# A hybrid decoder layer on one core: the first transfers of three stages reordered and split, and a reciprocal root taken as an exponential of a logarithm

## Chip, core and metric

One core of a Trainium2 chip. The metric is the device time of the whole program in microseconds (us), median of three runs. Engines: TensorE (PE, with its weight loads PEld), VectorE (DVE), ScalarE (ACT), GpSimd (POOL), and SyncE (SP), which issues all the DMAs that are spoken of here.

## What is computed

One layer on x of 2048 tokens by 1024 channels, and a final norm:

```python
h = rms_norm(x, norm_mix); proj = h @ w_in
o_a = gated linear attention; o_b = RG-LRU branch; o_c = dilated attention, then rms_norm
x = x + concatenate([o_a, o_b, o_c]) @ w_out
h = rms_norm(x, norm_ffn)
up = causal_dwconv(h @ ffn_w_up, ffn_conv_w, ffn_conv_b)
u_val, u_gate = split(up)
x = x + (u_val * gelu(u_gate)) @ ffn_w_down
return rms_norm(x, norm_final)       # x * rsqrt(mean(x*x) + EPS) * g
```

## The kernel before

Four stages follow each other: `mixer_front` (input projection, groups A and B), `dilated_attention` (group C), `output_projection` and `conv_ffn`. Each ends with a barrier of all engines, at which every DMA of the stage has landed; then the next stage's queues start. Within a stage every engine runs a list written out by hand, in order, and waits on semaphores. Data are held transposed, channels on the 128 partitions, and tokens come in four blocks of 512 (`NB`). All large products have float32 accuracy through splits: ACT copies an operand to `_hi`, DVE subtracts to get `_lo`, and PE makes three passes (L66 to L68; in the FFN L2035 to L2037) per 128 by 128 piece of weights and 512 tokens. The names begin with the stage: ip_, at_, op_, ff_.

**`dilated_attention`.** SP loads q, k and v of a block (`load_qkv`, L1292, 768 KB each), two identities (`idb`, `idf`), the masks, and then the other blocks. PE waits at its start for both identities and the masks, and at the first scores for q, k and v of block 0. `idf` and v are first used in `turn_values` (L1609), after the three score groups of the first tile.

**`output_projection`.** The weights come in four slabs of 256 columns (1 MB each, `w_raw`, two buffers), the mixed input in tiles of 128 by 512 (256 KB) through a ring of four (`mix_in`, `load_mix`, L1828). ACT makes `w_hi` of slab 0 (L1874), then `mix_hi` of the eight tiles of block 0 (L1882); DVE follows with `w_lo` (L1934) and `mix_lo` (L1939), which also frees a ring slot for SP. The first product (m = 0) waits for one `mix_lo` after the other. DVE adds each product to x (L1992), with four PSUM banks, so product n waits for addition n - 4; in each block DVE makes the next block's `mix_lo` of the same index first. ACT squares the sum, POOL adds the squares, PE sums over partitions, ACT takes the square root (`root`, L1894), and DVE the reciprocal (`invert`, L1944) into `rstd`, for blocks 0 to 2 in the middle of the next block, for block 3 at the stage's end. DVE then norms blocks 0 and 1 and forms differences of them (`norm`, `combine`) for the FFN, and stores go out to `h_t`.

**`conv_ffn`.** The up-projection uses a Strassen scheme of seven products for each of 22 slabs; the tokens are done in two halves of 1024. `ORDER` names products: A00, S1, S2, A01, S3, A00 of the next slab, A11, A01 of the next, S4, and so on. At the start SP loads seven inputs `b_raw` (1 MB each) from `h_t` and slab 0 (1 MB) after the first of them; ACT makes `b_hi` of one input and then one weight piece (`high_b`, `high_w`), seven times, and only after these the copies of product results (`keep`, L2448) that S2 waits for. Product A00 waits for all four pieces of its input. Between the halves, and at the end, comes the final norm of a half: squares, totals, `root(half, b)` for its two blocks (ACT square root, L2490), `invert(half)` on DVE (reciprocal L2645, then four multiplications L2649 per block), and stores. Between the halves PE goes on with products of half 1; its S4 waits for two moves on DVE (`move`, L2597, L2599), which wait for the four stores of half 0 (`late_stored`); A11 waits for ACT's copy of S3. At the end POOL multiplies the other half of the channels (L2408) beside DVE.

## Time and profile before

| | us |
|---|---|
| median of 3 runs (lowest, highest) | 2625.37 (2622.48, 2629.85) |
| profiled execution, own time | 2634.46 |
| span of the profiled execution | 2632.7 |
| PE busy | 2482.2 (94%) |
| DVE / ACT / POOL busy | 1582.7 / 1074.8 / 735.1 |

The profiled execution's time is 1.8 us more than its span. A row of the timeline gives the start from the span's beginning, the duration, and in brackets how long the engine sat idle before it and what released it. Matmuls are pipelined, so one of 0.39 us starts 0.23 us after the one before at full clock, and one of 0.63 us 0.43 us after it at half clock.

### The profile page before, as it was taken

The numbers are of one execution on the slowest core, as the hardware profiler recorded it, in microseconds if no ns is written. First come the engines' busy times: TensorE is split into PE (matmuls) and PEld (weight loads), VectorE is DVE, ScalarE is ACT, GpSimd is POOL, SyncE is SP. The second block draws the span as 40 slices with busy tenths as digits, with TensorE's granted clock in tenths as the row PEclk, the third lists the DMA queues.
The fourth block names the chain that finished last, engine by engine and source line by source line (L and its number), as shares of the span: only waits on it lengthen the run. The fifth ranks groups of instructions, "written<-read, shape, count | busy, mean of one in ns | idle before, by whom it ended". The sixth has DMA issues, their size and how long they took to land.

```text
span 2632.7 us, 32946 instructions
## 1 busy us (share of the span) xinstructions
PE 2482.2 (94%) x12224; PEld 2003.0 (76%) x12224; DVE 1582.7 (60%) x2166; ACT 1074.8 (41%) x1847; POOL 735.1 (28%) x648
## 2 busy tenths in 40 slices
PE   7999999999799996995999999899989999989995
PEld 5777777777578775874888888788868888878884
DVE  7554447774355674455777777445577877763435
ACT  6434353332146553213444444225444444432422
POOL 4111103331003770323333333012044534310103
PEclk9999989999899998997999999999999999999997
DMA  4232224442513325364212122365413222225472
GB/s 160 97 111 93 94 87 156 143 148 72 191 59 127 103 71 212 108 228 180 88 72 93 76 88 85 140 211 201 163 73 131 102 88 81 86 83 175 146 242 109
DMA packets 147199, 327.27 MB, mean 124 GB/s; under 512 B 12624, under 2 KB 54624, under 8 KB 139104
## 3 DMA queue, kind: packets, MB, share of 16 engines
q1 hardware_dynamic: 147040, 325.17, 35.4%
q8 instruction: 98, 1.61, 0.3%
q14 instruction: 61, 0.50, 0.1%
HBM read 231.55 MB, written 93.57 MB: 123 GB/s over the span
## 4 chain that ended last, share of the span: by engine, by line
PE 46%; DVE 3%; ACT 1%; DMA 1%; issue 1%; POOL 1%; SPq 0%; DVEq 0%; ACTq 0%; POOLq 0%
PE ff_bank L2035 16%; PE ff_bank L2037 15%; PE ff_bank L2036 15%; DVE ff_y L2618 1%; POOL ffn_rstd L2362 1%; DMA ff_b_raw<-h_t 1%; DVE ff_x2d L2649 1%; DVE ffn_rstd L2645 1%; DMA ff_a_raw<-a_t 0%; ACT ff_y L2457 0%; ACT ff_b_hi L2420 0%; DVE ff_x2d L2640 0%; DVE ff_a_lo L2632 0%; ACT ff_e L2448 0%; ACT ff_ring L2438 0%
## 5 line engine op out<-in xcount | busy, mean ns | idle before, releaser
L2035 PE MATMUL ff_bank<-ff_b_hi,ff_ring 128*128 128x512 f32 x1232 | 483.5, 392 | 37.3 <-DVE ff_ring L2580 15.8
L2036 PE MATMUL ff_bank<-ff_b_lo,ff_ring 128*128 128x512 f32 x1232 | 482.0, 391 | 0.0
L2037 PE MATMUL ff_bank<-ff_b_hi,ff_ring 128*128 128x512 f32 x1232 | 482.0, 391 | 0.0
L66 PE MATMUL ip_bank<-ip_x_hi,ip_w_hi 128*128 128x512 f32 x736 | 309.1, 420 | 19.4 <-DVE ip_x_lo L701 16.2
L2035 PEld LDWEIGHTS ff_bank<-ff_b_hi,ff_ring 128*128 128x128 f32 x1232 | 233.1, 189 | 90.4 <-issue 31.7
L67 PE MATMUL ip_bank<-ip_x_lo,ip_w_hi 128*128 128x512 f32 x736 | 298.8, 406 | 0.0
L68 PE MATMUL ip_bank<-ip_x_hi,ip_w_lo 128*128 128x512 f32 x736 | 297.4, 404 | 0.0
L2035 PE MATMUL ff_bank<-ff_a_hi,ff_w_hi 128*128 128x512 f32 x704 | 276.6, 393 | 15.5 <-DVE ff_a_lo L2632 15.4
L2618 DVE SCALAR_TENSOR_TENSOR ff_y<-ff_u,ff_conv_all,ff_y 128x1024 f32<-128x1024 f32 x176 | 240.2, 1365 | 62.8 <-ACT ff_y L2457 59.3
L2036 PE MATMUL ff_bank<-ff_a_lo,ff_w_hi 128*128 128x512 f32 x704 | 275.7, 392 | 0.0
L2037 PE MATMUL ff_bank<-ff_a_hi,ff_w_lo 128*128 128x512 f32 x704 | 275.4, 391 | 0.0
L2037 PEld LDWEIGHTS ff_bank<-ff_b_hi,ff_ring 128*128 128x128 f32 x1232 | 232.9, 189 | 48.7
L2036 PEld LDWEIGHTS ff_bank<-ff_b_lo,ff_ring 128*128 128x128 f32 x1232 | 233.0, 189 | 48.3 <-issue 0.2
L2580 DVE TENSOR_TENSOR ff_ring<-ff_raw,ff_ring 128x512 fp32r<-128x512 f32 x220 | 178.3, 812 | 56.5 <-ACT ff_ring L2438 56.5
L2630 DVE TENSOR_TENSOR ff_w_lo<-ff_w_raw,ff_w_hi 128x512 fp32r<-128x512 f32 x88 | 62.6, 712 | 243.6 <-ACT ff_w_hi L2471 243.6
L66 PEld LDWEIGHTS ip_bank<-ip_x_hi,ip_w_hi 128*128 128x128 f32 x736 | 145.4, 198 | 57.9 <-issue 14.8
L2471 ACT ACTIVATE ff_w_hi<-ff_w_raw 128x512 fp32r<-128x512 f32 x88 | 55.6, 631 | 302.9 <-PE ff_bank L2037 269.9
L67 PEld LDWEIGHTS ip_bank<-ip_x_lo,ip_w_hi 128*128 128x128 f32 x736 | 145.9, 198 | 32.0 <-issue 2.6
L68 PEld LDWEIGHTS ip_bank<-ip_x_hi,ip_w_lo 128*128 128x128 f32 x736 | 145.3, 197 | 32.1
L2035 PEld LDWEIGHTS ff_bank<-ff_a_hi,ff_w_hi 128*128 128x128 f32 x704 | 133.2, 189 | 45.7 <-DVE ff_a_lo L2632 17.5
L2457 ACT ACTIVATE ff_y<-ff_u,ff_conv_all 128x1024 f32<-128x1024 f32 x88 | 109.6, 1245 | 135.6 <-DVE ff_u L2601 101.1
L1440 ACT ACTIVATE at_probs<-at_s,at_neg 128x256 f32<-128x256 f32 (+1 forms) x288 | 107.8, 436 | 137.3 <-DVE at_neg L1521 123.5
(244 smaller groups left out, 4402.2 us busy)
## 6 DMA issues: line engine op xcount, KB each, us to landing
ff_raw<-in_slabs SPq DMA_DIRECT2D x44, 1024.0 KB, 4.8
ff_a_raw<-a_t SPq DMA_DIRECT2D x88, 512.0 KB, 4.1
proj_t<-ip_staged SPq DMA_DIRECT2D x92, 256.0 KB, 2.7
a_t<-ff_y SPq DMA_DIRECT2D x44, 512.0 KB, 2.7
ff_w_raw<-in_w_down SPq DMA_DIRECT2D x88, 256.0 KB, 2.7
rp_tables<-in_rope SPq DMA_DIRECT2D x24, 512.0 KB, 4.5
ip_w_raw<-in_w_in SPq DMA_DIRECT2D x23, 512.0 KB, 4.1
at_qkv<-proj_t SPq DMA_DIRECT2D x12, 768.0 KB, 12.1
```

The source lines that it names most:

```text
L66: pe.matmul(out, w_hi[k], x_hi[k], start=(k == 0), stop=False)
L67: pe.matmul(out, w_hi[k], x_lo[k], start=False, stop=False)
L68: last = pe.matmul(out, w_lo[k], x_hi[k], start=False, stop=(k == n - 1))
L1440: ins = act.activation(probs[:, g, at], scores_at(j, g)[:, hh, n * c:n * (c + 1)], ACT.Exp, bias=neg[:, j % 2, c, 2 * g + hh:2 * g + hh + 1])
L2035: pe.matmul(out, w_hi, x_hi, start=first, stop=False, skip_group_check=resumed)
L2036: pe.matmul(out, w_hi, x_lo, start=False, stop=False, skip_group_check=resumed)
L2037: return pe.matmul(out, w_lo, x_hi, start=False, stop=last, skip_group_check=resumed)
L2457: act.activation(y[:, a, :], u[:, a, TAPS - 1:], ACT.Identity, bias=conv_all[:, g, a, TAPS:TAPS + 1], scale=conv_all[:, g, a, TAPS - 1:TAP ...
L2471: act.activation(w_hi[n % 2][:, :], w_raw[n % 2][:, :], ACT.Copy).then_inc(d_hi_ready, 1)
L2580: dve.tensor_tensor(ring[:, M % RING, 1, :], source(half, m), ring[:, M % RING, 0, :].bitcast(F32), ALU.subtract).then_inc(w_lo_ready, 1)
L2618: dve.scalar_tensor_tensor(out=y[:, a, :], in0=u[:, a, t:t + HALF], scalar=conv_all[:, g, a, t:t + 1], in1=y[:, a, :], op0=ALU.mult, op1=A ...
L2630: dve.tensor_tensor(w_lo[n % 2][:, :], w_raw[n % 2][:, :], w_hi[n % 2][:, :].bitcast(F32), ALU.subtract).then_inc(d_lo_ready, 1)
```

## The change

Attention: the small identity and the masks are loaded first, then q, k, `idf`, v of block 0; PE's start waits for identity and masks, scores for q and k alone, `turn_values` for v and `idf`. Output projection: slab 0 comes in two halves of 128 columns (rows of 512 bytes), each split on its own; ACT and DVE do the first half, two tiles, the second half, then six tiles; product 0 waits for the first half. FFN: weight piece A00 of slab 0 is loaded and split ahead of everything, and products on slab 0 wait for one piece of input after the other. Both norms: ACT takes Ln and then Exp with scale -0.5, which gives the reciprocal root, and DVE's reciprocal is gone. A table set that holds both functions is loaded at the start of the output projection and ahead of the last eight squares.

```diff
@@ -1176,7 +1176,9 @@
         gain_in = sem("gain_in")
-        qkv_in = [sem(f"qkv_in{b}") for b in range(BLOCKS)]
+        mask_in = sem("mask_in")
+        qk_in = [sem(f"qk_in{b}") for b in range(BLOCKS)]
+        values_in = [sem(f"values_in{b}") for b in range(BLOCKS)]
...
 
         @block.sync
         def _(sp):
+            def load_one(b, a, t, landed):
+                sp.dma_start(qkv[:, a, :, blk(b)], proj_t[t:t + GROUPS, :, blk(b)].rearrange("g p s -> p g s")).then_inc(landed[b], 16)
+
             def load_qkv(b):
-                for a, t in enumerate((T_CQ, T_CK, T_CV)):
-                    sp.dma_start(qkv[:, a, :, blk(b)], proj_t[t:t + GROUPS, :, blk(b)].rearrange("g p s -> p g s")).then_inc(qkv_in[b], 16)
+                load_one(b, 0, T_CQ, qk_in)
+                load_one(b, 1, T_CK, qk_in)
+                load_one(b, 2, T_CV, values_in)
...
@@ -1332,10 +1338,12 @@
                 sp.wait_ge(out_ready, 4 * (b + 1))
                 sp.dma_start(mix_t[5:8, :, blk(b)].rearrange("g p s -> p g s"), out[:, b % 2, :, :]).then_inc(out_stored[b % 2], 16)
 
-            load_qkv(0)
-            sp.dma_start(idb[:, :], ident_bf).then_inc(consts_in, 16)
-            sp.dma_start(mask[:, :, :], masks).then_inc(consts_in, 16)
+            sp.dma_start(idb[:, :], ident_bf).then_inc(mask_in, 16)
+            sp.dma_start(mask[:, :, :], masks).then_inc(mask_in, 16)
+            load_one(0, 0, T_CQ, qk_in)
+            load_one(0, 1, T_CK, qk_in)
             sp.dma_start(idf[:, :], ident).then_inc(consts_in, 16)
+            load_one(0, 2, T_CV, values_in)
             sp.dma_start(gain[:, :], swa_gain).then_inc(gain_in, 16)
             for b in range(1, BLOCKS):
                 load_qkv(b)
...
@@ -1373,7 +1381,7 @@
                     pool.wait_ge(scores_ready, GROUPS * (j - 1))
                 elif j == TILES_0:
                     for b in range(BLOCKS):
-                        pool.wait_ge(qkv_in[b], 48)
+                        pool.wait_ge(qk_in[b], 32)
...
 
             def make_diagonal(i):
                 f = i - FIRST_1
+                if f == 0:
+                    pool.wait_ge(consts_in, 16)
                 pool.wait_ge(rstd_ready, f + 1)
...
@@ -1599,10 +1609,14 @@
 
         @block.tensor
         def _(pe):
-            pe.wait_ge(consts_in, 16 * 3)
+            pe.wait_ge(mask_in, 32)
             pe.wait_ge(cleared, 2)
 
             def turn_values(b):
+                if b % 4 == 0:
+                    pe.wait_ge(values_in[b // 4], 16)
+                if b == 0:
+                    pe.wait_ge(consts_in, 16)
                 if b:
                     pe.wait_ge(v_ready, b)
...
@@ -1816,7 +1833,11 @@
             def load_weights(n):
                 if n >= 2:
                     sp.wait_ge(w_ready, n - 1)
-                sp.dma_start(w_raw[:, n % 2, :, :], w_slabs[n]).then_inc(w_loaded[n % 2], 16)
+                if n == 0:
+                    sp.dma_start(w_raw[:, 0, :, 0:P], w_slabs[0, :, :, 0:P]).then_inc(first_loaded, 16)
+                    sp.dma_start(w_raw[:, 0, :, P:2 * P], w_slabs[0, :, :, P:2 * P]).then_inc(w_loaded[0], 16)
+                else:
+                    sp.dma_start(w_raw[:, n % 2, :, :], w_slabs[n]).then_inc(w_loaded[n % 2], 16)
...
@@ -1869,9 +1890,14 @@
 
         @block.scalar
         def _(act):
+            def first_high():
+                act.wait_ge(first_loaded, 16)
+                act.activation(w_hi[:, :, 0:P], w_raw[:, 0, :, 0:P], ACT.Copy).then_inc(first_hi_ready, 1)
+
             def weights_high(n):
                 act.wait_ge(w_loaded[n % 2], 16 * (n // 2 + 1))
-                act.activation(w_hi[:, :, n * 2 * P:(n + 1) * 2 * P], w_raw[:, n % 2, :, :], ACT.Copy).then_inc(w_hi_ready, 1)
+                skip = 0 if n else P
+                act.activation(w_hi[:, :, n * 2 * P + skip:(n + 1) * 2 * P], w_raw[:, n % 2, :, skip:], ACT.Copy).then_inc(w_hi_ready, 1)
...
@@ -1891,10 +1917,15 @@
 
             def root(b):
                 act.wait_ge(sum_done, b + 1)
-                act.activation(rstd[:, blk(b)], sum_bank[:, :], ACT.Sqrt, bias=eps[:, :], scale=1.0 / D).then_inc(std_ready, 1)
-
+                act.activation(rstd[:, blk(b)], sum_bank[:, :], ACT.Ln, bias=eps[:, :], scale=1.0 / D).then_inc(std_ready, 1)
+                act.wait_ge(std_ready, b + 1)
+                act.activation(rstd[:, blk(b)], rstd[:, blk(b)], ACT.Exp, scale=-0.5).then_inc(rstd_ready, 1)
+
+            act.preload_act_table_set("natural_log_exp_and_others")
+            first_high()
+            high(0, range(2))
             weights_high(0)
-            high(0, range(KT))
+            high(0, range(2, KT))
             for n in range(1, OUT_SLABS):
                 weights_high(n)
...
@@ -1928,10 +1959,15 @@
             dve.memset(ones[:, :], 1.0).then_inc(consts_ready, 1)
             dve.memset(eps[:, :], EPS).then_inc(consts_ready, 1)
 
+            def first_low():
+                dve.wait_ge(first_hi_ready, 1)
+                dve.tensor_tensor(w_lo[:, :, 0:P], w_raw[:, 0, :, 0:P], w_hi[:, :, 0:P].bitcast(F32), ALU.subtract).then_inc(first_ready, 1)
+
             def weights_low(n):
                 dve.wait_ge(w_hi_ready, n + 1)
-                at = slice(n * 2 * P, (n + 1) * 2 * P)
-                dve.tensor_tensor(w_lo[:, :, at], w_raw[:, n % 2, :, :], w_hi[:, :, at].bitcast(F32), ALU.subtract).then_inc(w_ready, 1)
+                skip = 0 if n else P
+                at = slice(n * 2 * P + skip, (n + 1) * 2 * P)
+                dve.tensor_tensor(w_lo[:, :, at], w_raw[:, n % 2, :, skip:], w_hi[:, :, at].bitcast(F32), ALU.subtract).then_inc(w_ready, 1)
...
-            def invert(b):
-                dve.wait_ge(std_ready, b + 1)
-                dve.reciprocal(rstd[:, blk(b)], rstd[:, blk(b)]).then_inc(rstd_ready, 1)
-
+            first_low()
+            low(0, 0)
+            low(0, 1)
             weights_low(0)
-            for k in range(KT):
+            for k in range(2, KT):
                 low(0, k)
             for n in range(1, OUT_SLABS):
                 weights_low(n)
...
                     dve.tensor_tensor(at, banks[n % 4][:, :], at, ALU.add).then_inc(added, 1)
-                    if b and m == 2:
-                        invert(b - 1)
                     if b in (1, 2) and m in (3, 4):
                         for k in range(KH * (m - 3), KH * (m - 2)):
                             norm(b - 1, k)
                     if b == 2 and m in (4, 5, 6, 7):
                         for k in range(KH):
                             combine((T1, T3, T2, T4)[m - 4], k)
-            invert(BLOCKS - 1)
             dve.wait_ge(rstd_ready, BLOCKS)
...
@@ -2016,7 +2048,9 @@
                     pe.wait_ge(mix_ready, KT * (b + 1))
                 for m in range(KT):
                     n = KT * b + m
-                    if b == 0 and m % 2 == 0:
+                    if n == 0:
+                        pe.wait_ge(first_ready, 1)
+                    elif b == 0 and (m == 1 or m % 2 == 0):
                         pe.wait_ge(w_ready, m // 2 + 1)
...
@@ -2202,7 +2237,10 @@
                 if G >= 2:
                     before, h = (g - 2, half) if g >= 2 else (g - 2 + PAIRS, half - 1)
                     sp.wait_ge(w_lo_ready, use_at(h, "S4", before) + 1)
-                sp.dma_start(raw[:, g % 2, :, :], slabs[g]).then_inc(slab_in[g % 2], 16)
+                if G == 0:
+                    sp.dma_start(raw[:, 0, 1:4, :], slabs[0, :, 1:4, :]).then_inc(slab_in[0], 16)
+                else:
+                    sp.dma_start(raw[:, g % 2, :, :], slabs[g]).then_inc(slab_in[g % 2], 16)
...
 
+            sp.dma_start(raw[:, 0, 0, :], slabs[0, :, 0, :]).then_inc(first_in, 16)
             load_h(B00)
             load_slab(0, 0)
...
@@ -2424,6 +2465,8 @@
                 G = PAIRS * half + g
                 if name[0] == "S":
                     act.wait_ge(s_ready, 4 * G + int(name[1]))
+                elif G == 0 and name == "A00":
+                    act.wait_ge(first_in, 16)
                 else:
                     act.wait_ge(slab_in[g % 2], 16 * (PAIRS // 2 * half + g // 2 + 1))
...
@@ -2487,14 +2530,19 @@
                 act.wait_ge(sum_done, 2 * half + b + 1)
                 if half and b == 0:
                     act.wait_ge(early_ready, 2 * OC)
-                act.activation(out_rstd[:, blk(b)], banks[SUM[b]][:, :], ACT.Sqrt, bias=eps[:, :], scale=1.0 / D).then_inc(std_ready, 1)
+                act.activation(out_rstd[:, blk(b)], banks[SUM[b]][:, :], ACT.Ln, bias=eps[:, :], scale=1.0 / D).then_inc(std_ready, 1)
+                act.wait_ge(std_ready, 2 * half + b + 1)
+                act.activation(out_rstd[:, blk(b)], out_rstd[:, blk(b)], ACT.Exp, scale=-0.5).then_inc(rstd_ready, 1)
 
             for half in range(HALVES):
                 if half == 0:
                     for i in range(7):
+                        if i == 0:
+                            high_w(0, 0)
                         for k in range(KH):
                             high_b(0, KH * i + k)
-                        high_w(0, i)
+                        if i:
+                            high_w(0, i)
                     act.wait_ge(consts_ready, 2)
...
@@ -2543,6 +2591,7 @@
                     square(0, 1, range(6, 8))
                     high_w(1, 8)
                 else:
+                    act.preload_act_table_set("natural_log_exp_and_others")
                     square(1, 1, range(8))
...
@@ -2641,8 +2690,6 @@
 
             def invert(half):
                 for b in range(HB):
-                    dve.wait_ge(std_ready, 2 * half + b + 1)
-                    dve.reciprocal(out_rstd[:, blk(b)], out_rstd[:, blk(b)]).then_inc(rstd_ready, 1)
                     dve.wait_ge(rstd_ready, 2 * half + b + 1)
                     for o in range(OC):
...
@@ -2652,9 +2699,12 @@
             for half in range(HALVES):
                 if half == 0:
                     for o in range(7):
+                        if o == 0:
+                            low_w(0, 0)
                         for i in range(4 * o, 4 * o + 4):
                             low_b(0, i)
-                        low_w(0, o)
+                        if o:
+                            low_w(0, o)
...
@@ -2713,8 +2763,6 @@
                 G = PAIRS * half + g
                 o, bank, first = {"A00": (B00, X, True), "S1": (T1, Y, True), "S2": (T2, X, False), "A01": (B10, Z, True),
                                   "S3": (T3, X, False), "A11": (T4, X, False), "S4": (B11, Y, False)}[name]
-                if g == 0:
-                    pe.wait_ge(b_lo_ready, 28 * half + 4 * (HI_AT[o] + 1))
                 pe.wait_ge(w_lo_ready, M + 1)
...
                 out = banks[bank[g % 2]][:, :]
                 for k in range(KH):
+                    if g == 0:
+                        pe.wait_ge(b_lo_ready, 28 * half + 4 * HI_AT[o] + k + 1)
                     cols = slice(k * P, (k + 1) * P)
```

SP's queue at the start of the attention; `at_qkv` is the tile of q, k and v. Before:

```order
L1292 DMA at_qkv<-proj_t 128x3x512 x3
L1336 DMA at_idb<-in_ident_bf 128x128
L1337 DMA at_mask<-in_masks 128x768
L1338 DMA at_idf<-in_ident 128x128
L1339 DMA at_gain<-in_swa_norm 128x3
L1292 DMA at_qkv<-proj_t 128x3x512 x9
```

and now:

```order
L1341 DMA at_idb<-in_ident_bf 128x128
L1342 DMA at_mask<-in_masks 128x768
L1293 DMA at_qkv<-proj_t 128x3x512 x2
L1345 DMA at_idf<-in_ident 128x128
L1293 DMA at_qkv<-proj_t 128x3x512
L1347 DMA at_gain<-in_swa_norm 128x3
L1293 DMA at_qkv<-proj_t 128x3x512 x9
```

v of block 0 and `idf` stand behind what PE's first scores need.

ACT between the two halves of the FFN; `ff_e` is a copy of a product, `ff_ring` holds split weights, `ffn_rstd` the reciprocal root. Before:

```order
L2448 ACTIVATE ff_e<-ff_bank 128x512
L2490 ACT_TABLE_LOAD
L2490 ACTIVATE ffn_rstd<-ff_bank,ff_eps 128x512 x2
L2438 ACTIVATE ff_ring<-ff_s_12793 128x512 x2
L2438 ACTIVATE ff_ring<-ff_raw 128x512
L2448 ACTIVATE ff_e<-ff_bank 128x512
```

and now:

```order
L2491 ACTIVATE ff_e<-ff_bank 128x512
L2533 ACT_TABLE_LOAD
L2533 ACTIVATE ffn_rstd<-ff_bank,ff_eps 128x512
L2535 ACT_TABLE_LOAD
L2535 ACTIVATE ffn_rstd<-ffn_rstd 128x512
L2533 ACT_TABLE_LOAD
L2533 ACTIVATE ffn_rstd<-ff_bank,ff_eps 128x512
L2535 ACT_TABLE_LOAD
L2535 ACTIVATE ffn_rstd<-ffn_rstd 128x512
L2481 ACTIVATE ff_ring<-ff_s_12806 128x512 x2
L2481 ACTIVATE ff_ring<-ff_raw 128x512
L2491 ACTIVATE ff_e<-ff_bank 128x512
```

One table load has become four here, since no set is loaded by hand in half 0.

SP's queue at the start of the output projection. Before:

```order
L1819 DMA op_w_raw<-in_w_out 128x2048
L1828 DMA op_mix_in<-mix_t 128x512 x4
L1819 DMA op_w_raw<-in_w_out 128x2048
L1828 DMA op_mix_in<-mix_t 128x512 x4
L1819 DMA op_w_raw<-in_w_out 128x2048
L1836 DMA op_x<-in_x_t 128x8x512
```

and now:

```order
L1837 DMA op_w_raw<-in_w_out 128x8x128
L1838 DMA op_w_raw<-in_w_out 128x8x128
L1849 DMA op_mix_in<-mix_t 128x512 x4
L1840 DMA op_w_raw<-in_w_out 128x2048
L1849 DMA op_mix_in<-mix_t 128x512 x4
L1840 DMA op_w_raw<-in_w_out 128x2048
L1857 DMA op_x<-in_x_t 128x8x512
```

Both halves of slab 0 still stand ahead of the input tiles; nothing behind them has moved.

## Rows read from the trace of the kernel before

**Rows 1.** The page: PE's granted clock in 40 slices of the span, tenths.
```profile
PEclk9999989999899998997999999999999999999997
```

**Rows 2.** Timeline, PE: start, busy us, engine, line, operation; idle before and its releaser.
```profile
701.36 0.61 PE L1627 MATMUL at_s<-at_mask,at_idb 128*128 128x256 bf16 x2 [14.68 <-DMA at_idf<-in_ident]
1022.01 0.77 PE L66 MATMUL op_bank<-op_mix_hi,op_w_hi 128*128 128x512 f32 x1 [15.64 <-DVE op_mix_lo L1939]
1049.09 0.47 PE L66 MATMUL op_bank<-op_mix_hi,op_w_hi 128*128 128x512 f32 x1 [1.73 <-DVE op_x L1992]
1163.34 0.50 PE L66 MATMUL op_bank<-op_mix_hi,op_w_hi 128*128 128x512 f32 x1 [3.38 <-DVE op_mix_lo L1939]
1227.75 0.77 PE L2035 MATMUL ff_bank<-ff_b_hi,ff_ring 128*128 128x512 f32 x1 [15.76 <-DVE ff_ring L2580]
1246.19 0.76 PE L2035 MATMUL ff_bank<-ff_b_hi,ff_ring 128*128 128x512 f32 x1 [10.16 <-ACT ff_e L2448]
1948.24 0.76 PE L2035 MATMUL ff_bank<-ff_b_hi,ff_ring 128*128 128x512 f32 x1 [8.60 <-DVE ff_u L2599]
```

**Rows 3.** Table of windows: span, PE, PEld, DVE, ACT, POOL busy, clock, DMA, GB/s.
```profile
696.00:701.00 5.00, 0.00 (x0) 0.00 (x0) 0.00 (x0) 0.00 (x0) 0.00 (x0) 0.50 1.03 356
```

**Rows 4.** Timeline at the projection's start: ACT, then SP.
```profile
1028.64 0.63 ACT L1882 ACTIVATE op_mix_hi<-op_mix_in 128x512 fp32r<-128x512 f32 x1 [1.33 <-DMA op_mix_in<-mix_t]
1046.91 2.46 ACT L1882 ACTIVATE op_mix_hi<-op_mix_in 128x512 fp32r<-128x512 f32 x4 [4.47 <-DMA op_mix_in<-mix_t]
1021.89 2.12 SPq L1828 DMA_DIRECT2D op_mix_in<-mix_t  x4
```

**Rows 5.** Timeline, DVE in block 2 of the projection.
```profile
1136.13 3.34 DVE L1944 RECIPROCAL ffn_rstd<-ffn_rstd 128x512 f32<-128x512 f32 x1
1143.78 0.68 DVE L1992 TENSOR_TENSOR op_x_third<-op_bank,op_x_third 128x512 f32<-128x512 f32 x1
1144.38 6.03 DVE L1958 SCALAR_TENSOR_TENSOR op_x<-op_x,op_gain,ffn_rstd 128x512 f32<-128x512 f32 x4
1162.61 0.68 DVE L1939 TENSOR_TENSOR op_mix_lo<-op_mix_in,op_mix_hi 128x512 fp32r<-128x512 f32 x1
```

**Rows 6.** Waits of the DMA queue, then DVE's timeline, at the projection's end.
```profile
SPq L1759 <- DMA x_t<-op_x: 6.3, 1, 6.3
1212.75 3.35 DVE L1944 RECIPROCAL ffn_rstd<-ffn_rstd 128x512 f32<-128x512 f32 x1 [3.94 <-ACT ffn_rstd L1894]
```

**Rows 7.** Timeline, ACT at the FFN's start.
```profile
1237.66 2.19 ACT L2420 ACTIVATE ff_b_hi<-ff_b_raw 128x512 fp32r<-128x512 f32 x4 [2.03 <-DMA ff_b_raw<-h_t]
```

**Rows 8.** Timeline, ACT in the mixer: a logarithm, a table load.
```profile
333.53 0.30 ACT L634 ACTIVATE gl_rstd<-gl_ss,ip_eps 128x4 f32<-128x4 f32 x1
333.84 1.28 ACT L636 ACT_TABLE_LOAD   x1
```

**Rows 9.** Timeline between the FFN's halves: ACT, then DVE.
```profile
1927.15 1.28 ACT L2490 ACT_TABLE_LOAD   x1
1931.52 0.60 ACT L2448 ACTIVATE ff_e<-ff_bank 128x512 f32<-128x512 f32 x1 [0.24 <-PE ff_bank L2037]
1938.60 2.74 DVE L2649 SCALAR_TENSOR_TENSOR ff_x2d<-ff_x2d,ff_gain,ffn_rstd 128x512 f32<-128x512 f32 x4
1944.95 0.69 DVE L2597 TENSOR_TENSOR ff_u<-ff_bank,ff_e 128x512 f32<-128x512 f32 x1 [3.01 <-DMA out_t<-ff_x2d]
```

**Rows 10.** Timeline at the end: ACT, DVE, POOL, SP.
```profile
2605.95 1.28 ACT L2490 ACT_TABLE_LOAD   x1
2611.36 5.75 DVE L2649 SCALAR_TENSOR_TENSOR ff_x2d<-ff_x2d,ff_gain,ffn_rstd 128x512 f32<-128x512 f32 x4
2596.83 11.19 POOL L2362 TENSOR_TENSOR ffn_rstd<-ffn_rstd,ff_squares 128x512 f32<-128x512 f32 x8 [94.62 <-ACT ff_squares L2481]
2611.46 6.76 POOL L2408 TENSOR_TENSOR ff_x_last<-ff_x_last,ffn_rstd 128x512 f32<-128x512 f32 x4 [3.44 <-DVE ffn_rstd L2645]
2627.70 0.47 SPq L2297 DMA_DIRECT2D out_t<-ff_x_last  x1
```

More of the change, by code:

```diff
@@ L1462, in stage_queries @@
                     for b in range(BLOCKS):
-                        act.wait_ge(qkv_in[b], 48)
+                        act.wait_ge(qk_in[b], 32)
                 if j >= TILES_0 + 2:
@@ L1616, in scores @@
                         if b % 4 == 0:
-                            pe.wait_ge(qkv_in[b // 4], 48)
+                            pe.wait_ge(qk_in[b // 4], 32)
                     else:
@@ L1788, in output_projection @@
         w_loaded = [sem(f"w_loaded{i}") for i in range(2)]
+        first_loaded = sem("first_loaded")
+        first_hi_ready = sem("first_hi_ready")
+        first_ready = sem("first_ready")
         w_hi_ready = sem("w_hi_ready")
@@ L2114, in conv_ffn @@
         b_lo_ready = sem("b_lo_ready")
+        first_in = sem("first_in")
         slab_in = [sem(f"slab_in{i}") for i in range(2)]
@@ L2323, in sums_of_slab @@
                 pool.wait_ge(slab_in[g % 2], 16 * (PAIRS // 2 * half + g // 2 + 1))
+                if G == 0:
+                    pool.wait_ge(first_in, 16)
                 if G:
```

## Prediction

> **What bounds the kernel now.** I read PE's timeline first, for PE is busy nearly everywhere; what a border costs is an idle stretch ahead of one matmul, and such a stretch names its releaser [rows 2]. Seven of them matter: 14.68 us at the attention's start, 15.64 and then 1.73 in the output projection's first block, 3.38 ahead of its last block, 15.76 and 10.16 at the FFN's start, 8.60 between the halves. After the last matmul comes a tail of DVE, POOL and stores [rows 10]. A first transfer made smaller helps only if nothing behind it is pinned by something else; so for each stretch I ask which arrival ends the next one. The parts below count time saved against the profiled execution, 2634.46 us (its span of 2632.7 and 1.8 around it). It lies 9.1 above the median of 2625.37; the savings are put on both alike.
>
> **Attention's start: 1.9.** PE waits for the last of 2304 KB of q, k, v and 288 KB of identities and masks [rows 2]. Now it waits for 1536 and 224 KB: 832 KB or 0.85 MB less, which at 356 GB/s [rows 3] is 2.4 us. The large transfers stand behind two small ones now; SP needs half a microsecond per issue (four in 2.12) [rows 4], up to 1.0 later in all, partly filled by the small ones. So 1.4 to 2.4, taken 1.9. v and `idf`, landed by about 701.4 as before, are wanted 5 us after the first scores, so at 704: no wait. The stage has no further idle stretch of PE in rows 2, so this passes through.
>
> **Projection's start: -0.6.** Before, PE's first product starts at 1022.01. Half a slab split on its own saves about half of ACT's and DVE's work there, some 2 us, and the product can start near 1020. But its eighth step needs the last input tile, whose load SP issues once DVE has freed a slot with the fourth `mix_lo`; SP's four loads end at 1024.0 and ACT gets that tile at 1028.64 [rows 4]. In the new order the second half of the slab (about 1.0 on ACT and 1.2 on DVE, half of what the whole took) stands ahead of the third and fourth tile, so that load goes out about 1 us later, not earlier. Behind it, product 4 is pinned: it starts at 1049.09 after 1.73 of waiting for an addition [rows 2], which on DVE stands behind a `mix_lo` of block 1, whose tile ACT waited for until 1046.91 [rows 4]. That tile comes after 10 MB of other loads, which the earlier start of PE doesn't hasten, and the loads behind the last tile start later too. Ends: 0.5 saved (the transfers ahead move up a little) to 1.3 lost (the whole delay reaches the pinned tile). Taken: 0.6 lost. The table load at the stage's start stands in ACT's wait for the slab and costs nothing; with PE's start at stake it would cost 1.28.
>
> **Ahead of the last block: 1.8.** PE waits 3.38 for the last `mix_lo` of block 3, at 1162.61 on DVE [rows 2, 5], and DVE works almost without a pause from the reciprocal up to it. The reciprocal of 3.34 at 1136.13 leaves that chain. What is late next: the addition of product 4, at 1143.78. Products end 5.44 apart (24 matmuls, 0.227 each), the last of the block at 1163.34 - 3.38 = 1159.96, so product 4 at 1143.64, and the addition can't move up by more than 0.1. What is left is indirect: the last tile's load also waited for DVE, so ACT's squares and POOL's additions begin some 3 us earlier and run less beside the four multiplications at 1144.38, which took 6.03 there and 2.74 where POOL is quiet [rows 5, 9]. Less than the 3.29 of that excess goes. Bounds 0.1 and 3.3, taken 1.8, the middle. The reciprocals of the other blocks lie in DVE time that PE doesn't wait for in rows 2.
>
> **Projection's end: 0.4.** The reciprocal [rows 6] runs from 1212.75 to 1216.10; an Exp on ACT of about 0.6 (an ACT pass over 512 columns takes 0.60 [rows 9]) takes its place, 2.7 less. But SP waits 6.3 for the last store of x2, issued until 1209.4, so until 1215.7 [rows 6]: what is late next. Bounds 0.3 to 0.4.
>
> **FFN's start: 0.** Product A00 gets its weights and first input piece earlier, by some 3 us. S2 doesn't: it waits for ACT's copy, which stands behind all seven inputs, and ACT waited 2.03 for the sixth until 1237.66 [rows 7], the seventh megabyte in the queue. The same bytes stand ahead of it after the change. PE's gap of 10.16 grows by what the gap of 15.76 loses. Cost up to 0.4, for one more DMA issue.
>
> **Between the halves: 3.5.** Before: two roots, then DVE's reciprocal and multiplications twice, ending at 1941.34; the store lands and the first move starts at 1944.95 [rows 9]; S4 runs at 1948.24. Now four table loads. One load before a logarithm runs 1.28 from 1927.15, and in the mixer a load begins 0.01 after the logarithm of 0.30 before it has ended [rows 8, 9]. So Ln 1928.45 to 1929.14, load, Exp to 1931.1, load, Ln, load, Exp to 1935.0 (0.69, 1.30, 0.62 and so on). DVE's second group of 2.74 ends at 1937.8, that is 3.5 earlier, and store, moves and S4 follow. What is late next: ACT's copy of S3 slips from 1931.52 to 1936.7, ready at 1937.3. A11 would have started at about 1934.1, waits 3.2, and the two products behind it end at 42.9, still before S4's new start of 1944.7. If the clock falls to 1.2 GHz in that wait, as it was after the stretches of 8.60 and more (first matmul 0.76, and 0.50 after 3.38 [rows 2]), they end near 1946.3 and 1.6 is lost. Bounds 1.9 to 3.9.
>
> The Trainium skill, page ScalarE: Activation LUTs, section What ACT_TABLE_LOAD costs, says that every switch costs a drain of about 1.38 us beside the 1.283. Rows 8 show no such gap; by the page the three added switches would take some 4.1 us more (an estimate), and this term would be near -0.6.
>
> **The tail: 6.1.** The table load behind the squares [rows 10] moves ahead of them into idle time, and Exp follows Ln: Ln 2605.95 to 2606.64, Exp to 2607.3; DVE's multiplications begin at 2607.35, not 2611.36 (4.0). Then no reciprocal stands between DVE's groups. POOL becomes the bound: its totals end at 2608.02 [rows 10], then eight multiplications at the 1.65 of its first four (6.76 together) [rows 10], until 2621.3. The last store goes out at 2621.4 instead of 2627.70: 6.3, less 0.2 because eight stores of 512 KB now fall closer. Bounds 4.0 (only the earlier start counts) and 6.5.
>
> **Sum.** 1.9 - 0.6 + 1.8 + 0.4 + 0 + 3.5 + 6.1 = 13.1 us. Profiled 2634.46 - 13.1 = 2621.4; median 2625.37 - 13.1 = **2612.3 us**. About 0.3%, or 7.9 us, is what a measurement of this kernel can tell from no change, so 2617.5 is the border.
>
> **Rivals.**
> - *The first starts pass through.* Projection +2.5, last block 3.3, FFN's start 2.9, the other terms at their better ends (2.4, 0.4, 3.9, 6.5): 21.9, time 2603.5. For it: PE does start earlier at all three. Against: the pinned arrivals of rows 4 and 7. 12%.
> - *The gains are small.* All terms at their worse ends: 1.4 - 1.3 + 0.1 + 0.3 - 0.4 + 1.9 + 4.0 = 6.0, time 2619.4. For it: DVE and POOL slow each other at the tail. 19%.
> - *A switch of tables costs twice its row* where activations depend on each other: three loads more at 1.3 each. DVE ends at 1941.7, the half border gives -0.4, sum 9.2, time 2616.2. Rows 8 speak against it. The page named above would have it so. 6%.
> - *Slower: the clock.* In a slice of the mixer the granted clock lies between 0.8 and 0.9 (the sixth digit, 329 to 395 us), in the attention's middle, 750 to 980, at 0.9 or more [rows 1]. If the shifted start gave the attention's 280 us a clock of 0.85, PE would need 49 us more, net 36 slower, 2648. It decides for slower beyond 0.3% below about 0.93 (280 us x 0.075 = 21). Nothing in the steady part is changed, so 3%.
>
> **Chances.** The forecast has 60%, its own range 2608 to 2617. Faster than 2617.5: the forecast, the first rival, two thirds of the third, and some of the second: 0.82. Within 0.3%: 0.15. Slower: 0.03. The range for 8 in 10 goes from 2606.0, leaving out most of the first rival, to 2619.5, which takes in the second.
>
> **What would show it.** PE's first scores 12 to 13 us after the mixer's last matmul; the projection's first product 2 us earlier but product 4 where it was relative to the stage's start; the stretch of 3.38 down to 1 to 2; S2 of slab 0 still 29 us after SP's first FFN load, with an idle stretch near 13 ahead of it; four loads of 1.28 between the halves, A11 waiting about 3, S4 3.5 earlier; DVE and POOL working side by side from 2608 to the end. I am wrong if product 4 or S2 move up with their starts, if the last block's stretch is gone or untouched, or if the table loads show gaps around them.

## The result, and the profile after

| | us |
|---|---|
| changed kernel, median of 22 runs | 2619.55 (2608.52 to 2629.14) |
| kernel before, the same comparison, 22 runs | 2633.83 (2622.48 to 2640.6) |
| ratio, 95% interval | 0.9946 (0.9934 to 0.9958) |
| profiled execution after: time, span, granted clock | 2608.52, 2606.7, 0.971 |
| profiled execution before: time, span, granted clock | 2634.46, 2632.7, 0.963 |

By the ratio the change saves 0.54% or 14.2 us (11.1 to 17.4); the forecast of the saving was 13.1. The forecast of the time was 2612.3 with a range to 2619.5, and the median is 2619.55. So the saving was met and the time was not, by 0.05 us beyond the range and 7.3 above the forecast: the kernel before reads 2633.83 in this comparison, 8.5 us above the 2625.37 on which the forecast stood. One later execution, of the kernel `combined` below, had a granted clock of 0.741 from end to end and took 3133 us; it is left out of every number here.

The two profiled executions differ by 26.0 us, far more than the ratio. The largest part of that is no work of the change. The table of windows (start and end, span, PE's busy time and instructions, clock, DMA share, GB/s) shows the mixer from 100 us to its last matmul, before and then after, and its code is the same in both:

```profile
100.00:686.68 586.68, 585.67 (x2928) 0.95 0.33 108
```
```profile
100.00:670.36 570.36, 567.86 (x2924) 0.98 0.35 111
```

16.3 us at a clock of 0.95 against 0.98, with PE busy nearly throughout. Whoever compares stages has to count from a mark inside each stage. PE's timeline of the changed kernel, with the rows that answer to [rows 2]:

```profile
683.40 0.58 PE L1641 MATMUL at_s<-at_mask,at_idb 128*128 128x256 bf16 x2 [13.04 <-DMA at_qkv<-proj_t]
1002.83 0.76 PE L66 MATMUL op_bank<-op_mix_hi,op_w_hi 128*128 128x512 f32 x1 [14.36 <-DVE op_mix_lo L1975]
1030.31 0.47 PE L66 MATMUL op_bank<-op_mix_hi,op_w_hi 128*128 128x512 f32 x1 [1.07 <-DVE op_x L2027]
1143.36 0.50 PE L66 MATMUL op_bank<-op_mix_hi,op_w_hi 128*128 128x512 f32 x1 [2.19 <-DVE op_mix_lo L1975]
1207.15 0.77 PE L2069 MATMUL ff_bank<-ff_b_hi,ff_ring 128*128 128x512 f32 x1 [13.54 <-DVE ff_b_lo L2624]
1228.44 0.76 PE L2069 MATMUL ff_bank<-ff_b_hi,ff_ring 128*128 128x512 f32 x1 [8.69 <-issue]
1919.94 0.47 PE L2069 MATMUL ff_bank<-ff_b_hi,ff_ring 128*128 128x512 f32 x1 [3.00 <-issue]
1927.62 0.47 PE L2069 MATMUL ff_bank<-ff_b_hi,ff_ring 128*128 128x512 f32 x1 [1.98 <-DVE ff_ring L2629]
```

The wait of 3.00 ahead of A11 (1919.94) is new, and S4 (1927.62) waits 1.98 instead of 8.60. Between the halves ACT, then DVE:

```profile
1909.92 1.28 ACT L2533 ACT_TABLE_LOAD   x1
1911.22 0.69 ACT L2533 ACTIVATE ffn_rstd<-ff_bank,ff_eps 128x512 f32<-128x512 f32 x1
1911.92 1.28 ACT L2535 ACT_TABLE_LOAD   x1
1913.22 0.64 ACT L2535 ACTIVATE ffn_rstd<-ffn_rstd 128x512 f32<-128x512 f32 x1
1913.87 1.28 ACT L2533 ACT_TABLE_LOAD   x1
...
1915.88 1.28 ACT L2535 ACT_TABLE_LOAD   x1
```
```profile
1917.84 2.74 DVE L2696 SCALAR_TENSOR_TENSOR ff_x2d<-ff_x2d,ff_gain,ffn_rstd 128x512 f32<-128x512 f32 x4 [1.21 <-ACT ffn_rstd L2535]
1924.36 0.69 DVE L2646 TENSOR_TENSOR ff_u<-ff_bank,ff_e 128x512 f32<-128x512 f32 x1 [3.19 <-DMA out_t<-ff_x2d]
```

They answer to [rows 9]. Each load begins within 0.02 us of the end of what stands before it, and the next function begins 0.02 after the load's 1.28. The drain of 1.38 us per switch that the Trainium skill states (page ScalarE: Activation LUTs, section What ACT_TABLE_LOAD costs) isn't on this chain, with each function depending on the one before: the trace disagrees. The tail, DVE, POOL and SP, answering to [rows 10]:

```profile
2588.25 13.05 DVE L2696 SCALAR_TENSOR_TENSOR ff_x2d<-ff_x2d,ff_gain,ffn_rstd 128x512 f32<-128x512 f32 x8 [6.43 <-ACT ffn_rstd L2535]
2589.03 13.39 POOL L2449 TENSOR_TENSOR ff_x_last<-ff_x_last,ffn_rstd 128x512 f32<-128x512 f32 x8
2602.45 0.37 SPq L2336 DMA_DIRECT2D out_t<-ff_x_last  x1
```

DVE and POOL work side by side to the end, at 1.63 and 1.67 us per tile, and the last store is issued as POOL ends.

### The profile page after: what moved, and what is told of

It reads as the page before. It is cut to its first block, busy times and chain, and to the rows that moved or that the text cites. A ratio compares the mean times of both kernels' runs of the same rounds, so it can differ in the third digit from the quotient of the medians.

```text
span 2606.7 us, 32959 instructions
## 1 busy us (share of the span) xinstructions
PE 2468.8 (95%) x12224; PEld 1991.9 (76%) x12224; DVE 1557.8 (60%) x2159; ACT 1083.9 (42%) x1859; POOL 736.3 (28%) x648
## 4 chain that ended last, share of the span: by engine, by line
PE 47%; DVE 3%; POOL 1%; ACT 1%; DMA 1%; issue 1%; SPq 0%; POOLq 0%; ACTq 0%; DVEq 0%
PE ff_bank L2069 16%; PE ff_bank L2071 16%; PE ff_bank L2070 16%; DVE ff_y L2667 1%; POOL ffn_rstd L2403 1%; DVE ff_b_lo L2624 1%; POOL ff_x_last L2449 0%; DMA ff_a_raw<-a_t 0%; DMA ff_b_raw<-h_t 0%; ACT ff_y L2500 0%; DVE ff_ring L2629 0%; DVE ff_x2d L2689 0%; DVE ff_a_lo L2681 0%; ACT ff_a_hi L2515 0%; DMA out_t<-ff_x2d 0%
## 5 line engine op out<-in xcount | busy, mean ns | idle before, releaser
L66 PE MATMUL ip_bank<-ip_x_hi,ip_w_hi 128*128 128x512 f32 x736 | 302.2, 411 | 19.5 <-DVE ip_x_lo L701 16.1
L67 PE MATMUL ip_bank<-ip_x_lo,ip_w_hi 128*128 128x512 f32 x736 | 292.5, 397 | 0.0
L68 PE MATMUL ip_bank<-ip_x_hi,ip_w_lo 128*128 128x512 f32 x736 | 291.4, 396 | 0.0
```

The lines of the kernel that those rows point to most:

```text
L66: pe.matmul(out, w_hi[k], x_hi[k], start=(k == 0), stop=False)
L67: pe.matmul(out, w_hi[k], x_lo[k], start=False, stop=False)
L68: last = pe.matmul(out, w_lo[k], x_hi[k], start=False, stop=(k == n - 1))
```

## The experiments

Each run left a profile, and every kernel has one form or the other of each border, so the borders can be read in many executions. All stretches below are counted from a mark in the same profile. T1 is the matmul between the halves that waits for POOL's total (1924.90 before, 1907.68 after), T2 the first such one at the end (2602.54 and 2583.58). In brackets stand the number of profiles and the range.

| us | as before | as changed |
|---|---|---|
| attention's first scores, behind the mixer's last matmul | 14.61 (4 profiles, 14.48 to 14.68) | 13.07 (9, 12.65 to 13.82) |
| projection: product 0, behind SP's first issue | 10.07 (5, 9.90 to 10.24) | 8.89 (8, 8.45 to 9.33) |
| projection: product 4, behind the same | 37.49 (5, 37.10 to 37.97) | 37.12 (8, 36.08 to 38.05) |
| idle ahead of the last block | 3.33 (3, 3.23 to 3.38) | 2.18 (9, 2.18 to 2.19) |
| FFN: S2, behind SP's first issue | 28.99 (5, 28.95 to 29.05) | 29.99 (7, 29.67 to 30.66) |
| FFN: in the first down stage, the matmul behind PE's wait of some 7 us, to the same one of half 1 ("down stage" below) | 688.5 (3, 688.1 to 688.9) | 685.9 (9, 684.7 to 687.1) |
| end of the span, behind T2 | 30.12 (3, 30.10 to 30.16) | 23.12 (9, 23.06 to 23.15) |

**1. The kernel before, again** (no edit).

> The kernel before, once more. Theory A (the level of a time is set by the clock that an execution happens to get, and the three times shown before the prediction were low ones): ratio 1.000 within 0.001, median between 2628 and 2638 and not 2625; in its profile the mixer, whose code no kernel changes, ends anywhere between 670 and 687 us (670.4 after the change, 686.7 before it), its granted clock going the other way. Theory B (the changed kernel also speeds up the mixer): the mixer ends at 686 to 687 again, and the median is near 2625 plus nothing.

Ratio 1.0001 (0.999 to 1.0013), median 2635.05 of 12 runs. Its mixer ended at 683.1. In all profiles of the study, the mixer, unchanged in every kernel, ended between 670.4 and 686.7. Over the 73 executions of the kernel before that came after the three shown, the median is 2633.3, and only 14 are as low as the highest of those three (2629.85). Theory A stands against Theory B. That all three were low by chance alone would happen about once in 140 times (14/73 three times over, an estimate), so why they were low isn't shown.

**2. The changed kernel, again** (no edit).

> The changed kernel, once more. Theory A: ratio 0.9946 within 0.001; the mixer ends anywhere between 670 and 687 us. From stage to stage, as in its first profile: first scores 13.0 us after the mixer's last matmul, product 4 of the projection 46.1 us after attention's last wait (47.0 before), end of the span 23.1 us after the first total's matmul (30.2 before). The slow clock behind the projection's last wait of 2.2 us (ten matmuls at 0.43 us instead of 0.23, 2.0 us lost) is there in some executions and not in others. Theory B: the mixer ends at 670 to 671 again, and that slow clock is always there.

Ratio 0.9958 (0.9941 to 0.9974), median 2623.8; the mixer ended at 682.9. Product 4 came 37.1 us after the first issue instead of 36.1, so the first profile's 0.9 at that place was scatter. Behind the projection's last wait the clock was full this time. Theory B falls.

**3. Roots alone.** In the kernel before, in both places:

```diff
-act.activation(rstd..., sum_bank..., ACT.Sqrt, bias=eps, scale=1.0 / D).then_inc(std_ready, 1)
-dve.reciprocal(rstd..., rstd...).then_inc(rstd_ready, 1)
+act.activation(rstd..., sum_bank..., ACT.Ln, bias=eps, scale=1.0 / D).then_inc(std_ready, 1)
+act.activation(rstd..., rstd..., ACT.Exp, scale=-0.5).then_inc(rstd_ready, 1)
```

with the table loaded ahead at the projection's start and ahead of the last eight squares.

> The kernel before, with the roots alone as exponential of a logarithm. By the terms as read from the two profiles: ahead of the last block 1.2 (or 3.2 if the slow clock doesn't come), the projection's end 0.2, between the halves 3.4, the tail 7.0, in sum 11.8, ratio 0.9955. Rival (the first transfers carry half of the gain): 7 us, ratio 0.9973. In the profile: product 0, product 4 and the FFN's S2 where the kernel before has them (9.9 and 37.1 us after the projection's first DMA issue, 29.0 us after the FFN's first).

Ratio 0.9943 (0.9926 to 0.9959): the roots carry the gain. By the profile: last block 1.2, projection's end 0.2, tail 7.0; but 1.3 between the halves and not 3.4. There the clock fell in the wait ahead of A11. PE's timeline:

```profile
1929.86 0.76 PE L2031 MATMUL ff_bank<-ff_b_hi,ff_ring 128*128 128x512 f32 x1 [3.00 <-ACT ff_e L2444]
1930.42 0.63 PE L2032 MATMUL ff_bank<-ff_b_lo,ff_ring 128*128 128x512 f32 x1
```

The same wait as after the change, 3.00 us, but the matmul behind it takes 0.76 instead of 0.47, and the next 6.6 us have a clock of 0.54.

**4. First transfers alone** (the changed kernel with square root and reciprocal as before).

> The changed kernel with square root and reciprocal as before, so only the first transfers and their order are changed. By the terms: attention's start 1.6, the projection's start 0.9, the FFN's start -0.9, so 1.6 us, ratio 0.9994. Rival (the first transfers carry half of the gain): 7 us, ratio 0.9973. In the profile: product 0 and product 4 of the projection 8.7 and 36.2 us after its first DMA issue, S2 29.8 us after the FFN's first; the stretch between the halves 8.6 and the end 30.2 us after the first total's matmul, as before.

Ratio 0.999 (0.9977 to 1.0002): 2.6 us at best estimate, nothing at the interval's end. Product 0 at 9.13, S2 at 29.7; product 4 at 38.0, where 36.2 was expected from the first profile's low value. The rival's 7 us is outside.

**5. One table load between the halves.** In the changed kernel:

```diff
                     square(0, 1, range(6, 8))
+                    act.preload_act_table_set("natural_log_exp_and_others")
                     high_w(1, 8)
```

> The changed kernel with the table that holds logarithm and exponential loaded in ACT's idle time ahead of the ninth slab copy of the second half, so one table load in place of four, off the chain. Theory A (the chain of ACT and DVE up to the last store of out_t sets S4): logarithm right behind ACT's copy, exponentials 1.3 and 2.7 later, DVE's second group ends near 9.0 us after the first total's matmul instead of 12.9, S4 at 16.0 to 16.6 instead of 19.9; A11 doesn't wait (3.0 now), and the chance of a slow clock behind that wait goes too. 3.4 to 3.9 us less than the changed kernel, ratio near 0.9938 where the changed kernel is 0.9952. Rival (S4 is next pinned by the loads of the slabs, ACT's copy waits 6.8 us for one): under 1 us.

Ratio 0.9952 (0.9937 to 0.9967), too wide to tell it from the changed kernel; the profile tells. S4 at 17.4 behind T1 instead of 19.9, the way from the first to the second down stage 682.5 instead of 685.3: 2.8 us, and no wait ahead of A11. The forecast of 3.4 to 3.9 was too much. DVE's timeline:

```profile
1926.74 6.76 DVE L2697 SCALAR_TENSOR_TENSOR ff_x2d<-ff_x2d,ff_gain,ffn_rstd 128x512 f32<-128x512 f32 x8 [0.62 <-ACT ffn_rstd L2535]
1937.43 0.69 DVE L2647 TENSOR_TENSOR ff_u<-ff_bank,ff_e 128x512 f32<-128x512 f32 x1 [3.33 <-DMA out_t<-ff_x2d]
```

The eight multiplications took 6.76 us and not twice 2.74; the first ones now run beside POOL's sums of a slab (until 1929.0), which is the likely reason but wasn't tried alone. The store's landing still holds the first move.

**6. The last multiplications on DVE.** POOL's loop over `x3_last` goes, and in DVE's `invert`, behind the four of each half:

```diff
+                    if half:
+                        if b == 0:
+                            dve.wait_ge(x3_in, 16 * (OC + 1))
+                        for o in range(OC):
+                            at = x3_last[:, o, blk(b)]
+                            dve.tensor_tensor(at, at, out_rstd[:, blk(b)], ALU.mult).then_inc(early_ready, 1)
```

> The changed kernel with the last eight multiplications on DVE, between its own, and none on POOL. Theory A (at the end the two engines slow each other: 1.63 and 1.67 us per tile side by side, 0.69 for one on DVE with POOL quiet): sixteen tiles at 0.6 to 0.69 from 4.7 us behind the first total's matmul, the last store issued at 15.0 instead of 18.9; eight stores of 512 KB then bind: the span ends 20.0 to 21.5 us behind that matmul instead of 23.1, so 1.6 to 3.1 less. Rival (POOL's multiplications were free, DVE's pace is its own): sixteen at 1.63, the end 13 us later.

Ratio 0.9947 (0.9929 to 0.9966). In the profile the end is 21.6 behind T2 instead of 23.1: 1.5 less, just under Theory A's 1.6 to 3.1. The rows, DVE and then SP's last:

```profile
2604.17 3.36 DVE L2689 SCALAR_TENSOR_TENSOR ff_x2d<-ff_x2d,ff_gain,ffn_rstd 128x512 f32<-128x512 f32 x4 [6.43 <-ACT ffn_rstd L2528]
2607.45 2.48 DVE L2696 TENSOR_TENSOR ff_x_last<-ff_x_last,ffn_rstd 128x512 f32<-128x512 f32 x4
2609.86 2.73 DVE L2689 SCALAR_TENSOR_TENSOR ff_x2d<-ff_x2d,ff_gain,ffn_rstd 128x512 f32<-128x512 f32 x4
2612.51 2.49 DVE L2696 TENSOR_TENSOR ff_x_last<-ff_x_last,ffn_rstd 128x512 f32<-128x512 f32 x4
```
```profile
2615.02 1.00 SPq L2336 DMA_DIRECT2D out_t<-ff_x_last  x1
```

Sixteen tiles on one engine in 10.8 us (2604.17 to 2615.0), where two engines side by side took 14.2 (2588.25 to 2602.4). The last store goes out 3.4 us earlier, but 6.1 us before the end instead of 4.3, since now the DMA engines are full. Windows of 3 us up to 3 us behind the last issue:

```profile
2612.20:2615.20 3.00, 0.00 (x0) 0.00 (x0) 2.80 (x5) 0.00 (x0) 0.00 (x0) 0.50 1.02 378
2615.20:2618.20 3.00, 0.00 (x0) 0.00 (x0) 0.00 (x0) 0.00 (x0) 0.00 (x0) 0.50 1.03 381
```

In the changed kernel they moved 307 and 306 GB/s there, at a share of 0.82.

**7. Block 3's low parts early.** In DVE's loop of the projection:

```diff
-                    if b + 1 < BLOCKS:
+                    if b + 1 < BLOCKS and not (b == 2 and m > 4):
                         low(b + 1, m)
+                    if b == 2 and m == 4:
+                        for k in range(5, KT):
+                            low(3, k)
```

> The changed kernel with the last three tiles of block 3 (low parts) taken ahead of the additions and differences of block 2 on DVE. Theory A (the stretch ahead of block 3 is DVE's order alone, ACT has the high parts 20 us earlier): the stretch of 2.2 goes, and with it the slow clock that follows it in some executions (1.6 us): 2.2 to 3.8 less than the changed kernel up to the last total, ratio near 0.9940. Rival (the additions behind it get late and PE waits for a bank instead): the stretch moves to product 4 of block 3, gain under 0.5.

Ratio 0.994 (0.9922 to 0.9958). The idle stretch ahead of block 3 is gone. From product 4 to the last total it is 158.1 us; the changed kernel had 162.2 in both its profiles, each with one fall of the clock worth 1.6, and seven other kernels without the reciprocal on DVE had 160.6 to 162.2. So 2.5 us are the edit's, and up to 4.1 with the clock. The wait was DVE's order: the edit changes nothing else.

**8. Two starts undone** (the changed kernel with the projection's slab whole and the FFN's first issues, splits and waits as before).

> The changed kernel with the slab of the projection whole again, and the first pieces and waits of the FFN as before; attention's start and the roots as changed. Theory A (these two starts bring PE forward but not what is pinned): S2 29.0 us after the FFN's first DMA issue instead of 29.8 to 30.7, product 4 of the projection at 37.1 to 38.0 as in all profiles but one; 0.7 to 1.7 less than the changed kernel. Rival (starts pass through): 2 to 3 us more than the changed kernel.

Ratio 0.9959 (0.9945 to 0.9973), not to be told from the changed kernel by the time. S2 at 29.0, product 4 at 37.5: PE's earlier starts bring these two nothing, and S2 is 1.0 earlier without them.

**9. The FFN's first input ahead of the small piece:**

```diff
-            sp.dma_start(raw[:, 0, 0, :], slabs[0, :, 0, :]).then_inc(first_in, 16)
             load_h(B00)
+            sp.dma_start(raw[:, 0, 0, :], slabs[0, :, 0, :]).then_inc(first_in, 16)
```

> The changed kernel with the FFN's first input issued ahead of the small piece of the slab. Theory A (S2 comes 0.9 us later because the small piece first leaves the DMA engines half idle: 235 GB/s in the second 2 us against 434): S2 at 29.0 to 29.3 us after the FFN's first DMA issue instead of 29.8 to 30.7, product A00 at 8.5 to 9.0 as now. Rival (the extra issue or the many small packets cost it): S2 stays at 29.8.

S2 at 29.3, product A00 at 8.6. This one profile has S2 0.7 below the mean of the seven in the table and 0.3 below the lowest of them, so some of the loss of 1.0 comes back. Ratio 0.9926 (0.9903 to 0.9949), four runs. The windows of the third and fourth microsecond behind the first issue, before and then after:

```profile
1219.22:1221.22 2.00, 0.00 (x0) 0.50 1.04 434
```
```profile
1200.61:1202.61 2.00, 0.00 (x0) 0.50 0.83 235
```

In those 2 us 0.4 MB less came in, and ACT gets the input that it waits for (20.4 us behind the first issue before, 21.3 after) 0.9 us late. S2 came where Theory A had it (29.0 to 29.3), but the trace of `input_first` doesn't bear out its reason. There the third to sixth microsecond read:

```profile
1209.80:1211.80 2.00, 0.00 (x0) 0.50 0.98 410
1211.80:1213.80 2.00, 0.00 (x0) 0.50 0.86 209
```

The dip has only moved to where the small piece now stands (the kernel before has 401 GB/s in the fifth and sixth). Six microseconds behind the first issue, 1.40 MB had come in, 1.46 after the change and 1.84 before. The shares of 0.83 and 0.86 say that the DMA engines weren't half idle but slow: by the trace's packet records the piece's 128 packets of 2 KB took 0.19 us each on the mean after the change and 0.17 here, while packets of four times their size took some 0.31. So the rival, that the small packets or the extra issue cost it, isn't ruled out, and why S2 came somewhat earlier all the same stays open.

**10 and 11. The waits by step.** By then the clock behind A11's wait of 3.0 us was full in four profiles, all with the waits by step of the changed FFN, and low in two without them (the expectation counts `half_preload` as a fifth, which has no such wait). `one_wait` puts one wait back in the changed kernel, `roots_step_waits` puts the waits by step into kernel 3:

```diff
-                if g == 0:
-                    pe.wait_ge(b_lo_ready, 28 * half + 4 * (HI_AT[o] + 1))
...
                 for k in range(KH):
+                    if g == 0:
+                        pe.wait_ge(b_lo_ready, 28 * half + 4 * HI_AT[o] + k + 1)
```

> The changed kernel with one wait ahead of a first product of the FFN, as before, in place of one wait for each step. Theory A (the waits by step keep the clock up through the 3.0 us idle stretch ahead of A11 between the halves: clock 1.00 in the five profiles with them, 0.50 behind the stretch in the two without): clock 0.50 behind it, 686.7 us from the FFN's first to its second down stage instead of 685.3, 1.4 us slower than the changed kernel. Theory B (chance): clock 1.00 behind it and 685.3.

> The kernel before with the new roots, and one wait for each step in the first products of the FFN. Theory A (the waits by step keep the clock): clock 1.00 behind the stretch of 3.0 us and 685.3 us from the first to the second down stage, where the kernel without them had 0.50 and 686.9. Theory B (chance, or something else of the changed start): 0.50 and 686.9 stay.

Both go against Theory A. `one_wait` had the full clock and 685.2; `roots_step_waits` had 0.78 in the 7.6 us behind the stretch, and 686.8. `input_first`, which has the waits by step, had 0.61 and 687.1. Ratios 0.9941 (0.992 to 0.9963) and 0.9961 (0.9945 to 0.9977). Six profiles had looked like a rule and weren't: the same wait of 3.0 us lowers the clock in four of nine executions, with and without these waits.

**12. All together** (5, 6 and 7, with the FFN's first issues and splits as before).

> The changed kernel with the three single edits together (one table load between the halves, the last multiplications on DVE, block 3's low parts early) and the FFN's first DMA issues and splits as before. If the gains add: 2.8 + 1.5 + 3.5 + 0.9 = 8.7 us less than the changed kernel (14 less than the kernel before), ratio 0.9915 within 0.0015. Rival (each edit only moves the wait to the next one): ratio 0.9940 as of the single edits. In the profile: 205 us from attention's last wait to the last total of the projection, S2 at 29.0, S4 17.4 us behind the first total between the halves, the end 21.6 behind the first total of the tail.

Median 2608.0 of five runs, ratio 0.9915 (0.9897 to 0.9933): as the sum has it. Its profile is that of the execution left out above, so the single places weren't read. By the median it is the fastest of the study. Its interval ends just below where that of the changed kernel begins (0.9933, 0.9934), but overlaps that of `input_first`.

## Why the prediction was right and wrong

**The level: wrong.** The step that failed is the last sentence of its first part, "It lies 9.1 above the median of 2625.37; the savings are put on both alike", and the range built on it. The three times shown were low ones: 73 later executions have a median of 2633.3. The profiled execution at 2634.46 was the ordinary one, and 2634.46 - 13.1 = 2621.4 stood in the text. The range held only what the terms leave open. It had nothing for the level, though one of the four times at hand lay 4.6 above the highest of the other three. What the level goes with is the granted clock: the changed kernel's 22 runs go from 2608.5 at 0.971 to 2629.1 at 0.962, with the same code. What makes an execution's clock wasn't tried.

**Attention's start: right**, 1.5 of 1.9, inside its bounds, and it passes through: from the first scores to attention's last wait it is 300.6 to 302.6 us in either form.

**Projection's start: direction not met.** 0.6 lost was forecast, 0.4 saved is the mean, and the scatter of product 4 is 2 us, so neither is shown. Product 0 moved by 1.2 and not by 2. A part of the working was incomplete: it followed the eighth tile's issue, which is later, and left out that SP's issue of the fifth tile waits for the first `mix_lo`, which is earlier (8.5 us behind the first issue instead of 9.9) and fills DMA time that had been open (10 to 12 us behind the first issue 351 GB/s instead of 191). That product 4 is pinned by a tile and not by PE's start holds.

**Ahead of the last block: right in kind, 1.2 and not 1.8.** The four multiplications took 5.86 instead of 6.03, so the excess that was to go [rows 5] stayed; the gain came from the differences behind them. "Taken 1.8, the middle" had no row. And kernel 7 shows what was overlooked: the high parts were there 20 us earlier, and moving three instructions is worth 2.5 or more.

**Projection's end: 0.2** instead of 0.3 to 0.4, held by the store's landing as said.

**FFN's start: wrong by size.** "The same bytes stand ahead of it after the change" was true, but they come later: 0.4 MB less in the first six microseconds. 1.0 was lost, where at most 0.4 was allowed for one more issue. Product A00 came 1.5 earlier on the mean and not 3, and the idle stretch "near 13" ahead of S2 is two, of 2.70 and 8.69, since PE now starts, stops once more and waits again.

**Between the halves: right.** S4 came 3.4 earlier for 3.5 forecast, A11 waits 3.0 for 3.2, the table loads cost their rows and no more. The clock was named as the way to lose 1.6, and in four profiles of nine about that was lost (686.9 against 685.2 on the mean). The mean saving over both is 2.5.

**The tail: 7.0, above its bounds** of 4.0 to 6.5. The last store's issue was 6.3 earlier, as worked out, and POOL was the bound. The 0.2 that closer stores were to cost had the wrong sign: the end came 4.3 behind the last issue instead of 5.0.

The measured terms add up to 1.5 + 0.4 + 1.2 + 0.2 - 1.0 + 2.5 + 7.0 = 11.8 us, inside the intervals of both comparisons (11.1 to 17.4, and 6.8 to 15.5). That this lies so near the forecast of 13.1 is partly luck: the tail gave 0.9 and the projection's start 1.0 more than their terms, and the other places together 3.2 less. The first rival, starts that pass through, is refuted by kernels 4 and 8; the table rival by the trace; the slower one didn't come. Its time of 2648 was added up wrongly: 36 above the kernel before is 2661, and 2648 takes the saving off twice.

## What to carry to other kernels

A forecast of a time is a forecast of a level and of a difference: check the level against every execution at hand, the profiled one too, and give it its own share of the range. A first transfer made smaller moves the first product and little else; look for the arrival that pins the second, and count what the piece itself costs those behind it, here 0.4 MB less in six microseconds wherever it stood. Where an engine waits for the last of several inputs that have long been prepared, look at the order of instructions on the engine between them before looking for cheaper instructions.

## What was not expected of the hardware

- The clock falls in part of the executions behind one and the same idle stretch: after 3.0 us ahead of A11 in four of nine, after the projection's 2.2 us in two of nine and after its 3.3 in two of three. Where it fell, 7.6 us behind A11's wait had 0.60 to 0.78 instead of 1.00.
- It also falls while the profile shows PE busy without a pause. Windows of the mixer from 300 to 400 us, same code though not quite the same instructions, before and after:

```profile
300.00:400.00 100.00, 100.00 (x526) 0.90 0.24 79
```
```profile
300.00:400.00 100.00, 100.00 (x592) 1.00 0.31 99
```

- Two engines side by side were slower than one: 16 tiles in 10.8 us on DVE alone, in 14.2 on DVE and POOL together. The Trainium skill, page Perfetto Trace Analysis, section Optimizing Scalar/DVE Operations, says that moving work from DVE to GpSimd might not help because they share a port; the trace agrees: the division cost 3.4 us up to the last store's issue, of which 1.5 are left at the end of the span.
